# Normalising stages: an unscaled tile times a diagonal on TensorE in place of a scaled tile that is transposed

## The reference

```python
def rmsnorm(x, g):
    x32 = x.astype(F32)
    y = x32 * lax.rsqrt(jnp.mean(x32 * x32, axis=-1, keepdims=True) + NORM_EPS) * g.astype(F32)
    return y.astype(x.dtype)

for l in range(DEPTH):
    g = norm_g[l]
    x = x + rmsnorm(mixer(rmsnorm(x, g[0])), g[1])
    mk, mv = mem_kv(mem, mem_norm_g[l], w_xk[l], w_xv[l])        # rmsnorm of the memory rows inside
    x = x + rmsnorm(cross_attend(rmsnorm(x, g[2]), mk, mv, w_xq[l], w_xo[l]), g[3])
    x = x + rmsnorm(sq_relu_mlp(rmsnorm(x, g[4]), w_ff1[l], w_ff2[l]), g[5])
```

## Time and profile before

| | |
|---|---|
| runs | 4331.84, 4341.72, 4342.35 us; median 4341.72 |
| profiled execution | span 4337.2 us (no other time of it is listed) |
| TensorE | 3653.4 us busy, 84% of the span |
| TensorE's weight loads | 2941.7 us, 68% |
| VectorE | 1919.7 us, 44% |
| ScalarE | 1329.1 us, 31% |
| GpSimd | 122.3 us, 3% |

### The profile page before, as it was taken

How to read it: one execution, slowest core, us unless ns; L and a number is a source line. 1 busy time by engine, 2 the same in 40 slices (tenths; PEclk the granted TensorE clock), 3 DMA queues, 4 the chain that set the end, 5 groups by cost and what they waited for, 6 DMA issues and landing times. The chain is left out here.

```text
span 4337.2 us, 45172 instructions
## 1 busy us (share of the span) xinstructions
PE 3653.4 (84%) x17641; PEld 2941.7 (68%) x17641; DVE 1919.7 (44%) x3397; ACT 1329.1 (31%) x2116; POOL 122.3 (3%) x136
## 2 busy tenths in 40 slices
PE   6869926896788799999997998675868979999997
PEld 5734613435578699898885764563748869989887
DVE  3556997403232544445443310443523254444544
ACT  4342105432232422323334310211323242232332
POOL 0011200122000000000000000000000000000000
PEclk9989968998886799999998999555889679999999
DMA  2013100145130133333431100001122023333343
GB/s 79 16 45 82 27 1 1 51 134 175 49 102 30 53 128 131 114 123 117 143 129 39 44 20 21 1 4 38 44 68 88 25 102 117 136 117 116 127 145 118
DMA packets 223064, 336.08 MB, mean 77 GB/s; under 512 B 33205, under 2 KB 161821, under 8 KB 222882
## 3 DMA queue, kind: packets, MB, share of 16 engines
q1 hardware_dynamic: 211106, 291.63, 19.9%
q0 software_dynamic: 11776, 41.95, 3.0%
HBM read 323.06 MB, written 10.19 MB: 77 GB/s over the span
## 5 line engine op out<-in xcount | busy, mean ns | idle before, releaser
L198 PE MATMUL ps<-mlp_xl,s_mlp_w1h 128*128 128x384 f32 (+1 forms) x1536 | 504.1, 328 | 59.9 <-DVE s_mlp_w1l L575 59.9
L199 PE MATMUL ps<-mlp_xh,s_mlp_w1l 128*128 128x384 f32 (+1 forms) x1536 | 500.6, 326 | 0.0
L200 PE MATMUL ps<-mlp_xh,s_mlp_w1h 128*128 128x384 f32 (+1 forms) x1536 | 499.3, 325 | 0.0
L579 DVE TENSOR_TENSOR s_mlp_w2l<-s_mlp_w2b,s_mlp_w2h 128x1024 fp32r<-128x1024 f32 x192 | 235.3, 1225 | 536.2 <-ACT s_mlp_w2h L529 535.4
L199 PE MATMUL ps<-s_mlp_w2h,s_mlp_hl 128*128 128x512 f32 x1152 | 450.5, 391 | 0.0
L198 PE MATMUL ps<-s_mlp_w2l,s_mlp_hh 128*128 128x512 f32 x1152 | 449.5, 390 | 0.0
L200 PE MATMUL ps<-s_mlp_w2h,s_mlp_hh 128*128 128x512 f32 x1152 | 449.3, 390 | 0.0
L529 ACT CAST s_mlp_w2h<-s_mlp_w2b 128x1024 fp32r<-128x1024 f32 x192 | 201.4, 1049 | 598.6 <-PE ps L200 598.6
L198 PEld LDWEIGHTS ps<-mlp_xl,s_mlp_w1h 128*128 128x128 f32 x1536 | 292.9, 191 | 67.8 <-DVE s_mlp_w1l L575 61.3
L199 PEld LDWEIGHTS ps<-mlp_xh,s_mlp_w1l 128*128 128x128 f32 x1536 | 292.9, 191 | 6.5
L200 PEld LDWEIGHTS ps<-mlp_xh,s_mlp_w1h 128*128 128x128 f32 x1536 | 292.6, 190 | 0.0
(11 more groups left out here) (499 smaller groups left out, 6222.9 us busy)
## 6 DMA issues: line engine op xcount, KB each, us to landing
s_mlp_w1b<-w_ff SPq DMA_DIRECT2D x96, 1024.0 KB, 5.4
s_mlp_w2b<-w_ff SPq DMA_DIRECT2D x96, 1024.0 KB, 7.4
x_kb<-cache_mem_k SPq DMA_DIRECT2D x16, 512.0 KB, 7.2
x_vb<-cache_mem_v SPq DMA_DIRECT2D x2, 4096.0 KB, 21.1
s_orows_raw<-w_in_odd SPq DMA_DIRECT2D x32, 256.0 KB, 3.4
s_convsel_w<-w_in_even SPq DMA_DIRECT2D x12, 512.0 KB, 3.9
x<-x_prompt SPq DMA_DIRECT2D x1, 4096.0 KB, 12.8
ev_mixT<-w_in_even SPq DMA_DIRECT2D x16, 256.0 KB, 3.5
```

The source lines that it names most:

```text
L198: nc.tensor.matmul(out, ah, bl, start=first, stop=False, skip_group_check=True)
L199: nc.tensor.matmul(out, al, bh, start=False, stop=False, skip_group_check=True)
L200: return nc.tensor.matmul(out, ah, bh, start=False, stop=last, skip_group_check=True)
L579: nc.vector.tensor_tensor(w2l[:, j % 2], w2b[:, j // FC % 2, j % FC, :], w2h.bitcast(F32)[:, j % 2], ALU.subtract).then_inc(low2, 1)
```

## The change

The scaling on ScalarE falls away. In its place ScalarE makes one 128x128 diagonal matrix for each tile, `diag[:, t, :]`, from the identity matrix and the tile's column of inverse roots. TensorE multiplies the unscaled tile `src` with it: the tile is the stationary operand as before, and the moving operand is the diagonal instead of the identity; the product is the tile turned and scaled. The instruction is an ordinary `matmul` in place of a `transpose`. ScalarE runs two diagonals ahead of the tile that it looks at, and takes over the eviction of the tiles with t % 3 == 1, that is 1, 4 and 7 of nine and 1 of two, in eight instructions of 128 columns each, with the chunk's gain as scale; VectorE evicts the others as before. For that ScalarE waits for the gain vector ahead of its third diagonal, and for the turned halves of its tiles. `row_scaled` becomes `spread`, and `kept` is parted into `kept_dve` and `kept_act`: one semaphore more in each stage.

```diff
+    on_act = [t % 3 == 1 for t in range(n)]
-        scaled = S.sb("scaled", [P, 2, D])
+        diag = S.sb("diag", [P, n, P])
...
             act.wait_ge(inverted, 1)
+            for t in range(min(2, n)):
+                nc.scalar.activation(diag[:, t, :], G.ident[:], ACT.Copy, scale=stat[:, t:t + 1]).then_inc(spread, 1)
+            act.wait_ge(gain_in, 16)
             for t, r in enumerate(rows):
-                if t >= 2:
-                    act.wait_ge(turned, 2 * (t - 1))
-                nc.scalar.activation(scaled[0:r, t % 2, :], src[0:r, t, :], ACT.Copy,
-                                     scale=stat[0:r, t:t + 1]).then_inc(row_scaled, 1)
+                if t + 2 < n:
+                    nc.scalar.activation(diag[:, t + 2, :], G.ident[:], ACT.Copy, scale=stat[:, t + 2:t + 3]).then_inc(spread, 1)
+                if on_act[t]:
+                    for k in range(KD):
+                        i = 2 * t + k // 4
+                        if k % 4 == 0:
+                            act.wait_ge(turned, i + 1)
+                        ins = nc.scalar.activation(dst[:, k, t * P:t * P + r], G.ps[:, i % 8, (k % 4) * P:(k % 4) * P + r],
+                                                   ACT.Copy, scale=gT[:, k:k + 1])
+                        if k % 4 == 3:
+                            ins.then_inc(kept_act, 1)
...
-                pe.wait_ge(row_scaled, t + 1)
+                pe.wait_ge(spread, t + 1)
                 for hf in range(2):
                     i = 2 * t + hf
-                    if i >= 8:
-                        pe.wait_ge(kept, i - 7)
+                    if t >= 4:
+                        pe.wait_ge(kept_act if on_act[t - 4] else kept_dve,
+                                   2 * sum(on_act[u] == on_act[t - 4] for u in range(t - 4)) + hf + 1)
                     for k in range(4):
                         kk = 4 * hf + k
-                        ins = nc.tensor.transpose(G.ps[:, i % 8, k * P:k * P + r],
-                                                  scaled[0:r, t % 2, kk * P:(kk + 1) * P], G.ident[0:r, 0:r])
+                        ins = nc.tensor.matmul(G.ps[:, i % 8, k * P:k * P + r], src[0:r, t, kk * P:(kk + 1) * P],
+                                               diag[0:r, t, 0:r], start=True, stop=True)
                     ins.then_inc(turned, 1)
...
             for t, r in enumerate(rows):
+                if on_act[t]:
+                    continue
                 for hf in range(2):
...
-                                            ALU.mult).then_inc(kept, 1)
+                                            ALU.mult).then_inc(kept_dve, 1)
```

More of the change, by code:

```diff
@@ L136, in stage_norm @@
         junk = S.sb("junk", [P, D])
-        scaled = S.sb("scaled", [P, 2, D])
+        diag = S.sb("diag", [P, n, P])
         rs = S.sb("rs", [P, n])
-        gain_in, squared, meaned, rooted, inverted, row_scaled, turned, kept = (
-            S.sem(s) for s in ("gain_in", "squared", "meaned", "rooted", "inverted", "row_scaled", "turned", "kept"))
+        gain_in, squared, meaned, rooted, inverted, spread, turned, kept_dve, kept_act = (
+            S.sem(s) for s in ("gain_in", "squared", "meaned", "rooted", "inverted", "spread", "turned", "kept_dve", "kept_act"))
         block = S.open()
```

## The result

The changed kernel takes 4362.81 us (median of four runs, 4359.81 to 4364.34) against 4339.14 (four runs, 4331.84 to 4342.35). The ratio is 1.0057, with a 95% interval of 1.0042 to 1.0071: slower by 0.6%. The profiled execution took 4361.35 us, 4359.2 of them its span, against the span in the earlier trace rows.

A forecast was written before the change was run, and what follows sets the result against it. It took full stages as paced by transposes at half clock, then by VectorE and ScalarE, and after the change by TensorE throughout; 27.5 - 3.0 - 1.1 + 5.2 = +28.6 us on the median 4341.72 gave 4370 us, range 4351 to 4386.

The forecast's parts named there:

- Two records per plain f32 matmul: New matmul line: each plain f32 matmul takes two records where a transpose takes one; a tile 0.93 to 1.79 us.
- TensorE, first to last, in the four full stages: Nine-tile stages n0a, nx twice, n1a: TensorE's first to last work, together 74.0 us against 46.5, +27.5 us.
- X: Full stages: us run at half clock, 4.5 or 5.4 per stage, each adding 0.48 us; 18.9 in all.
- The earlier start: Full stages: TensorE starts 0.46 us after the first diagonal instead of 1.20 after ScalarE; -0.74 us each, -3.0 in all.
- The shorter end: Full stages: only a short last eviction, about 0.4 us, follows TensorE instead of some 0.7; -1.1 us in all.
- nm: The two-tile stage, run twice: 5.60 us becomes 7.6 and 8.8, with ScalarE's evictions last; +2.0 and +3.2, +5.2 us.
- The waits that end nothing: ScalarE's new waits for the gain vector and its tiles, and the extra semaphore: none ends last, nothing added.
- The sum against the median: Whole time: +28.6 us added to the median of the runs shown, 4341.72, 4.5 us above the profiled span.
- One record per matmul: Rival, new matmul line: a matmul costs what a transpose does; -2.4 us per full stage, -10 in all, 4332; 3%.
- A stage at half clock throughout: Rival: full stages stay at half clock, 31 us each against 11.6; +80 us in all, 4421; 5%.
- A matmul at the price of four transposes: Rival, new matmul line: a transpose is worth four plain passes; about +100 us, 4442; 3%.
- The clock carried over: Rival, the four following stages: the longer dense run leaves the clock up; up to -10 us, so +18, 4360; 5%.

The follow-up runs named there:

- e2: The kernel before with its transposes against the identity made plain matmuls, all else as before; 4366.47 us against 4337.59 (ratio 1.0067).
- e1: The changed kernel with its matmul turned back into a transpose against the identity, scaling by the inverse roots left out; 4326.76 us against 4337.59 (ratio 0.9971).
- e5_after: The changed kernel once more, without edits; 4366.46 us, one run.
- e3: The changed kernel with all evictions on VectorE, none on ScalarE; 4355.26 us against 4337.59 (ratio 1.0045).
- e4_warm: The changed kernel with 40 plain identity matmuls on TensorE ahead of n0a's and n1a's own work; 4359.15 us against 4337.89 (ratio 1.0045).
- e7_before_warm: The kernel before with 40 plain identity matmuls on TensorE ahead of the transposes in n0a and n1a; 4335.31 us, one run.

## Why the prediction held, step by step

The forecast was +28.6 us and 4370; measured were 4362.8 and a difference of 23.7 us between the medians, with the six stages longer by 29.1 and 26.9 us in the two pairs of traces. By its own steps, first trace against first trace:

- *Two records per plain f32 matmul.* Held, and it is the whole cause: e2 has the loss with this edit alone, e1 loses it with this edit undone.
- *TensorE, first to last, in the four full stages.* Forecast 74.0 us; measured 19.30 + 17.91 + 18.90 + 19.07 = 75.2. The price per record held at the full clock (0.113 us against 0.1115), and the short tile is not cheaper, as counted. The term that was off is X, the time at half clock: 4.5, 4.5, 4.5 and 5.4 us were forecast; the windows give 5.2 in n1a, 3.1 in the first nx and 5.5 in the second, and n0a's 19.30 us imply (19.30 - 16.23) / 0.48 = 6.4. Together 20.2 us instead of 18.9, 0.6 us in the sum; one stage alone was off by up to 2 us of X, that is by 1 us. That the sum came out this near is in part luck: X was 1.9 us too short for n0a and 1.4 too long for the first nx, and e5_after's four stages take 73.5 us. The other 0.6 us are the records' slightly larger distance.
- *The earlier start.* -3.0 forecast; 1.20 to 0.45 us is -0.75 per stage, -3.0.
- *The shorter end.* -1.1 forecast; what is left of a stage after TensorE's last went from about 0.9 to 0.6 us, -1.3 in all.
- *nm.* +2.0 and +3.2 forecast; +2.7 and +2.1 measured. Which of the two would stay cold was guessed the wrong way round, so that the sum held, 4.7 against 5.2, is luck. ScalarE's tail held (e3).
- *The waits that end nothing.* Held. In the first nx the third diagonal came right behind the gain vector, and TensorE did not stop; e1 shows what it looks like when such a wait does end last.
- *The sum against the median.* It was added to a median of three runs; the fourth run took that from 4341.7 to 4339.1. The 4.5 us between span and median were not all a difference of runs, since a time lies some 2 us above its own span (4361.35 against 4359.2). The remaining 5 us between 28.6 and 23.7 are within what the rest of the span moves by itself.

The rivals. One record per matmul was to give -10 us, -2.4 in each full stage. Its condition was not met, and its price was too large: in e1, which makes it so, the full stages are 0.7 to 1.0 us shorter than in the first trace of before and all six together 3.2. TensorE takes 10.85 us in n1a from first to last, not 10.2, and ScalarE's evictions lengthen the end, which that price had counted as shorter. That e1's median lies 10.8 us under the kernel before, near the -10, is a coincidence as far as the traces show. A stage at half clock throughout did not happen: the windows of n1a show the rise after 5.2 us. A matmul at the price of four transposes did not either: its two records cost 0.226 us at the full clock, and a transpose 0.107 (eight in a row whose weight loads take 0.86 us, the PEld row of e1), about half. The Trainium skill, "TensorE: Matmul & The Clock Gate", section Terms, gives transpose mode a factor of four for FP32. For these 128x128 tiles the trace shows about two. The clock carried over: the first matmul of the stage after n1a in the two kernels, before and changed:

```profile
2332.41 0.77 PE L198 MATMUL ps<-s_orows_wl,s_orows_sh 128*128 128x512 f32 x1 [7.87 <-DVE s_orows_wl L2197]
```

```profile
2346.70 0.77 PE L212 MATMUL ps<-s_orows_wl,s_orows_sh 128*128 128x512 f32 x1 [7.31 <-DVE s_orows_wl L2211]
```

The gap is 0.56 us shorter and the matmul as slow as before, 0.77 us. After both nx stages of the changed kernel it takes 0.66 us, as in the earlier trace rows. So the clock was not carried over.

## What to carry to other kernels

An idle-looking engine is no room for work before the work is counted in that engine's own records: a plain f32 matmul here is two weight loads and two matmul records where a transpose is one of each, so folding a scaling into the transpose doubled TensorE's records in the stage and made it the bound. Read the balance in the stage that is edited, at both clock levels: TensorE waited in the second half of these stages, but by 0.26 us per tile (1.19 against 0.93), and the edit asked for 0.86 more. And when a whole time moves by less than the sum of its stages, look at the same program twice before explaining the difference.

## What the runs showed of the hardware that was not expected

- The clock column says 1.00 over n0a's first 6.3 us in the changed kernel, while 30 records there take 0.21 us each, the pace that line 2014 has at 0.50 (0.215). In the first tens of us of an execution the column is thus no sure witness; the records' distances are:

```profile
36.10:42.40 6.30, 6.28 (x30) 1.00 0.00 0
```

- In n0a, after the same 40 matmuls, the work began at the full clock behind 2.03 us of idling in e4_warm (16.23 us for 142 records) and at half clock behind 3.38 us in e7_before_warm (0.54 in the first 3.7 us).
- The xs stages have several lengths. In the ten traces they took 62.8, 66.3 and 68.8 us, or values close to these, with transposes and with plain matmuls, and 59.8 in e3_all_dve; each of the two alone moves the whole time by up to 0.2%.
